# Hybrid decoder trunk on one core: the root's table load, a unit's end ahead of the weights' low part, and the attention's first loads at other slots

## The reference

```python
h = rmsnorm(x, g_pre) * (1 + scale) + shift          # scale, shift, gate from c @ w_ada
p = h @ w_in                                         # 1024 x 8704, split by columns
y_pool = pool_mixer(a_in, ...) * silu(a_g)
y_hgrn = hgrn2_mixer(b_q, b_f, b_i, ...) * silu(b_g)   # o = rmsnorm(o, norm_g) at its end
y_conv = short_conv_mixer(c_x, c_b, c_c, conv_w) * silu(c_g)
y_diff = diff_attention(d_q, d_k, d_v, ...) * silu(d_g)
merged = sum(sigmoid(m_g[n]) * (y_n @ w_merge_n) for n in range(4))
x = x + gate * rmsnorm(merged @ w_out, g_post)

# diff_attention, for each of 4 heads and each block of 128 queries
p = softmax(where(mask, q @ k.T * scale, NEG))       # two maps, m = 0 and 1
a = p[0] - lam_full * p[1]
o = rmsnorm(a @ v, norm_g) * (1 - lam_init)
```

## Time and profile before

| | us |
|---|---|
| median of 3 runs | 2526.8 |
| lowest, highest | 2520.53, 2531.47 |
| profiled execution | 2521.85 |
| its span, first to last instruction | 2520.0 |

### The profile page before, as it was taken

How to read it: one execution, slowest core, us unless ns; L and a number is a source line. 1 busy time by engine, 2 the same in 40 slices (tenths; PEclk the granted TensorE clock), 3 DMA queues, 4 the chain that set the end, 5 groups by cost and what they waited for, 6 DMA issues and landing times. The chain is left out here.

```text
span 2520.0 us, 35158 instructions
## 1 busy us (share of the span) xinstructions
PE 2264.2 (90%) x11572; PEld 1863.6 (74%) x11572; DVE 1429.2 (57%) x2638; ACT 1143.3 (45%) x2400; POOL 822.4 (33%) x739
## 2 busy tenths in 40 slices
PE   3598799898999889899999999999999967899998
PEld 2486677777777668687888888878888846677776
DVE  5676566655887777412776666445555434444452
ACT  3553455544544544422666666433434233434341
POOL 0113223323745654300232222123434216243342
PEclk7899999999999989999999999999999978999999
DMA  6699877758767666989564664487777777587781
GB/s 228 255 351 333 260 227 244 227 195 284 267 241 254 233 223 243 336 269 270 175 189 145 176 178 153 150 264 245 235 234 250 216 237 188 163 196 188 171 212 59
DMA packets 383963, 564.75 MB, mean 224 GB/s; under 512 B 32432, under 2 KB 248880, under 8 KB 382768
## 3 DMA queue, kind: packets, MB, share of 16 engines
q1 hardware_dynamic: 315248, 313.01, 42.8%
q10 hardware_dynamic: 68544, 249.59, 28.5%
HBM read 331.28 MB, written 231.21 MB: 223 GB/s over the span
## 5 line engine op out<-in xcount | busy, mean ns | idle before, releaser
L1682 PE MATMUL gb<-h_hi,w_both 128*128 128x512 f32 x1904 | 785.9, 413 | 89.2 <-ACT o L949 40.8
L1684 PE MATMUL gb<-h_hi,w_both 128*128 128x512 f32 x1904 | 755.1, 397 | 0.0
L1683 PE MATMUL gb<-h_lo,w_both 128*128 128x512 f32 x1904 | 754.0, 396 | 0.0
L1682 PEld LDWEIGHTS gb<-h_hi,w_both 128*128 128x128 f32 x1904 | 365.1, 192 | 173.0 <-issue 94.0
L1684 PEld LDWEIGHTS gb<-h_hi,w_both 128*128 128x128 f32 x1904 | 364.2, 191 | 80.8
L1683 PEld LDWEIGHTS gb<-h_lo,w_both 128*128 128x128 f32 x1904 | 365.7, 192 | 66.5
L949 ACT ACTIVATE o<-gb 128x512 f32<-128x512 f32 x272 | 161.5, 594 | 368.0 <-PE gb L1684 312.6
L809 POOL TENSOR_TENSOR C_prob<-C_prob,C_cf 128x512 f32<-128x512 f32 (+3 forms) x160 | 157.2, 1007 | 502.1 <-DVE C_cf L1358 488.1
L1014 ACT ACTIVATE C_prob<-C_sc,C_negm 128x512 f32<-128x512 f32 (+3 forms) x320 | 198.7, 622 | 245.4 <-DVE C_negm L1336 237.6
L1250 DVE TENSOR_TENSOR o<-gb,o 128x512 f32<-128x512 f32 x204 | 140.3, 688 | 228.7 <-PE gb L1684 218.0
L1240 DVE TENSOR_TENSOR w_both<-w,w_both 128x512 fp32r<-128x512 f32 x170 | 142.0, 836 | 173.4 <-ACT w_both L922 173.2
(11 more groups left out here) (230 smaller groups left out, 3711.7 us busy)
## 6 DMA issues: line engine op xcount, KB each, us to landing
wS_scratch<-w_both ACTq DMA_DIRECT2D x238, 512.0 KB, 4.4
w_both<-wS_scratch ACTq DMA_DIRECT2D x238, 512.0 KB, 4.3
w<-in_w_in_dram SPq DMA_DIRECT2D x68, 512.0 KB, 5.2
gT_scratch<-o SPq DMA_DIRECT2D x128, 256.0 KB, 4.7
D_gate<-gT_scratch SPq DMA_DIRECT2D x32, 1024.0 KB, 9.7
pT_scratch<-o SPq DMA_DIRECT2D x80, 256.0 KB, 4.2
C_qt<-qB_scratch SPq DMA_DIRECT2D x128, 128.0 KB, 3.6
C_ks<-kT_scratch SPq DMA_DIRECT2D x48, 256.0 KB, 5.7
```

Of the source, the lines that this page charges most:

```text
L1682: mm(to, hi[:, k, :], h_hi[j][:, k, :], start=(fresh and k == 0), stop=False, skip_group_check=True)
L1683: mm(to, hi[:, k, :], h_lo[j][:, k, :], start=False, stop=False, skip_group_check=True)
L1684: last = mm(to, lo[:, k, :], h_hi[j][:, k, :], start=False, stop=(k == KH - 1), skip_group_check=True)
```

## The change

Three edits, all in the first half. SyncE's five parts of the attention's first loads go from slots 45 to 49 to slots 39, 41, 43, 45 and 47 (the second half's stay). ScalarE's `root_h` gets an explicit load of the set with Ln and Exp for blocks 0 to 7, and `logs` drops its own for blocks 2 to 7. VectorE's end of a unit moves, within its slot, from behind `low(n+3)` and what follows it to directly ahead of `low(n+3)`, for the first step that the slot lists.

```diff
+BEGIN = ((39, 2), (279, 1))
...
                 for half in range(HALVES):
-                    if 0 <= n - ATTENTION[half][0] + 5 < 5:
-                        begin_attention(half, n - ATTENTION[half][0] + 5)
+                    part, odd = divmod(n - BEGIN[half][0], BEGIN[half][1])
+                    if not odd and 0 <= part < 5:
+                        begin_attention(half, part)
...
                 if i:
                     act.wait_ge(fin_done, i)
+                if i < MIX_HALF:
+                    act.preload_act_table_set("natural_log_exp_and_others")
                 link(a(rs[:, :, :], b7[:, 2:4, :], ACT.Ln, bias=epsb[:, :]))
...
                 i = mix_step(n, -9)
                 if i is not None:
-                    act.preload_act_table_set("natural_log_exp_and_others")
+                    if not 2 <= i < MIX_HALF:
+                        act.preload_act_table_set("natural_log_exp_and_others")
                     logs(i)
...
+            def end_units(half, s):
+
+                i = finished(half, s, 1)
+                if i is not None:
+                    factors(i)
+                i = None if half else finished(half, s, GATE)
+                if i is not None:
+                    gate_out(i)
+                i = finished(half, s, ON)
+                if i is not None:
+                    normalise(i)
...
+                taken = [hs for hs in att_slot(n)[:1] if hs[0] == 0]
+                for half, s in taken:
+                    end_units(half, s)
                 if n + LEAD < KEPT:
                     low(n + LEAD)
...
                 for half, s in att_slot(n):
-                    i = finished(half, s, 1)
-                    if i is not None:
-                        factors(i)
-                    i = None if half else finished(half, s, GATE)
-                    if i is not None:
-                        gate_out(i)
-                    i = finished(half, s, ON)
-                    if i is not None:
-                        normalise(i)
+                    if (half, s) not in taken:
+                        end_units(half, s)
                     z = piece(half, s)
```

## The result

The changed kernel takes 2482.21 us (median of 4 runs, 2480.70 to 2485.43); the kernel before took 2523.66 us beside it (4 runs, 2519.43 to 2531.47). The ratio is 0.9831, 95% interval 0.9818 to 0.9845: 41.5 us less. The profiled executions have spans of 2480.7 and 2520.0 us, 39.3 less. The forecast was 2488 with 2473 to 2509; measured against the 2526.8 it started from, the ratio gives 2484. So the total came out nearly as forecast. Its terms came out less well, as the stages show.

The account below looks back on a forecast made before the run. TensorE (PE), busy 90% of the span and working in program order, was taken as the bound. Gains of 10 + 7 + 22 = 39 us brought the median from 2526.8 to 2488 us, range 2473 to 2509.

Parts of the forecast that it names:

- Part 1: Slots 39 to 50: earlier first loads end PE's wait for causal_r in slot 50; -10 us, bounds -13 and +4.
- The 3 us put back for the collision: Slots 39 to 50: transfers moved earlier take 40 us where PE needs 37, so 3 us of the gain are lost.
- SyncE reaches the later kT stores when their `o` is ready: Slot 50: the store no longer queues behind loads, so 10.8 us of wait and 2.3 of clock, 13.1 us, can go.
- a wait under 1 us: Slot 50: the sign of the loads' move working, PE's wait for causal_r under 1 us, with full clock through the slot.
- Part 2: First half's mixers: one table load less ahead of the root shortens PE's stalls; -7 us, bounds 0 and -18.
- Part 3: First half's attention: a unit's end ahead of low removes PE's waits for y_out and on; -22 us, bounds -27 and +6.
- the sum over the 25 waits: First half's attention: idle time ahead of low plus low, against PE's wait; 25.5 of the 27.1 us go.
- for whatever comes late next: First half's attention: 3.5 us taken off the gain of the unit's end move for the next late result.
- Collision: Before slot 50: earlier loads fill the DMA engines and PE stands there instead; part 1 gives nothing, 2500 us; chance 0.14.
- Loop: First half's attention: ScalarE and VectorE, not PE, set the pace; part 3 gives 8 of its 22, 2502 us; chance 0.12.
- Interface: First half's attention: GpSimd's multiply stretches low by at most 1.0 us in 32 units; 2515 us; chance 0.06.
- Slower: First half's attention: y_out waits for PE's turn_back and holds VectorE's later work, 1.1 us a step; 2566 us; chance 0.04.

Follow-up runs that it names:

- only_a: The kernel before with only the attention's first loads moved to slots 39 to 47; 2518.33 us, ratio 0.9975.
- the five executions: Five profiled executions that run the changed kernel's very program up to the end of slot 50; slots 39 to 50 take 41.3 to 43.7 us.
- only_b: The kernel before with only the table loads changed: one load at the root, six left out at logs; 2514.05 us, ratio 0.9958.
- only_c: The kernel before with only a unit's end moved ahead of low in the first half's attention; 2492.55 us, ratio 0.9874.
- early_mask: The changed kernel with VectorE's two copies at the attention's beginning (ident_r, causal_r) in slot 47 instead of 50; 2478.99 us, ratio 0.9811.
- the fillers: The changed kernel with idle maxima added on VectorE: two behind low, two ahead of the unit's end, or one behind low; ratios 1.0047, 0.9940, 0.9906.
- outputs_ahead: The changed kernel with only y_out and on ahead of low, the factors behind it again; ratio 0.9845.
- fill_one: The changed kernel with one idle maximum on VectorE behind low in each of the 52 steps that end something; ratio 0.9906.
- root_only: The changed kernel with the six table loads at logs put back; 2476.57 us, ratio 0.9815.
- bunch39: The changed kernel with the attention's first loads one a slot at 39 to 43, not every second slot; 2482.13 us, ratio 0.9823.
- its half: The changed kernel with only the factors ahead of low, y_out and on behind it; ratio 0.9872.

## Why the prediction was right, and where its terms were not

**What bounds the kernel** held. Nothing gained in the first half was given back in a wait of the second: its attention took 440.8 us against 439.7.

**Part 1, forecast -10, measured -5.0** (6.8 in `only_a`, whose time fell by 6.3 us, 0.0025 of 2526.43; 6.8 as well between the mean of the five executions, 42.1, and that of the three with the old order, the kernel before, `only_b` and `only_c`, 48.9). The 3 us put back for the collision are about right: slots 39 to 49 take 35.8 us in the mean of the five and 32.4 in that of the three. The failed step is "SyncE reaches the later kT stores when their `o` is ready", taken to end the whole wait and bring the clock back with it, 13.1 us of slot 50's 17.1. SyncE does reach them in time (the store goes out at 261.52, as VectorE's `o` is done, 260.82 and 0.68), and slot 50 gives 11.5 us in four of the five. Two terms were left out: VectorE's own work ahead of the mask copy, 1.45 us of PE's wait in those four, and the two buffers of `hb`, which in the changed kernel's profile (5.4 us to landing) leave 3.59 of the 10.80 us, with the clock in slot 50 at 0.82, not 1. The prediction's own sign for this, a wait under 1 us, failed in all five. `early_mask` shows that the wait in slot 50 can be had; whether part of it comes back in slot 46 (3.53 us there, 1.22 to 3.30 in the five) its one profile doesn't tell.

**Part 2, forecast -7, measured -8.5** (6.3 in `only_b`). The forecast lies in the middle of what the stage shows: the kernels with part 2 take 446.2 to 449.5 us in it, the three without it (the kernel before, `only_a`, `only_c`) 454.6 to 455.8. The mechanism is as put: one load of 1283 ns ahead of the root, and nothing on PE's path at `logs`. PE's waits for ScalarE's copies in this stage fell by 7.9 us, the kernel before and then the changed one:

```profile
PE gb L1682 <- ACT o L949: 13.6, 6, 3.6
PE gb L1696 <- ACT o L952: 5.7, 5, 2.3
```

The loads of the changed kernel by line in its mixers (before: 8 at each of the three places), and two rows of PE's timeline behind roots:

```profile
L1111 ACT ACT_TABLE_LOAD x8 | 10.3, 1283 | 0.2
L1215 ACT ACT_TABLE_LOAD x2 | 2.6, 1283 | 0.0
```

```profile
651.52 0.53 PE L1696 MATMUL gb<-h_hi,w_both 128*128 128x512 f32 x1 [2.28 <-ACT o L952]
...
896.91 0.47 PE L1696 MATMUL gb<-h_hi,w_both 128*128 128x512 f32 x1 [3.40 <-DVE o L1256]
```

The first stall fell from 3.55 to 2.28 us, by 1.27. Not every stall that was counted moved: the one at 938.51, 3.40 us for VectorE, is 3.40 still, while the one a product ahead of it fell from 2.52 to 1.10. The Trainium skill's 2.66 us for a switch ("ScalarE: Activation LUTs", What ACT_TABLE_LOAD costs) would have made 14 us by the prediction's count; the first stall shows one load and no drain behind it, and the stage agrees with 1.28 a load.

**Part 3, forecast -22, measured -32.0.** The step that failed is a term of the sum. The idle time went as the sum over the 25 waits had it: PE's idle time of at least 0.1 us in this stage fell from 27.5 to 1.7 us, by 25.8, where the prediction had 25.5. Then it took 3.5 us off "for whatever comes late next"; nothing came. And it left out that PE's work gets shorter too: 261.18 us busy became 254.97 for the same 1412 matmuls. Of these 6.2 us some 1.8 are the clock. After the longest wait, 2.89 us to 533.28, it fell in the kernel before (columns as in the earlier trace rows):

```profile
530.00:535.00 5.00, 2.11 (x13) 1.65 (x12) 2.72 (x7) 1.67 (x3) 0.08 (x1) 0.94 0.61 232
535.00:540.00 5.00, 5.00 (x23) 4.19 (x23) 1.21 (x3) 1.16 (x3) 0.00 (x0) 0.71 0.66 220
```

A granted clock of 0.71 over 5 us is 2.9 us at the lower level of the two (1.2 of 2.4 GHz); 0.94 over the 5 us before is 0.6 more. In these 3.5 us half the work is done, so 1.8 are lost. The changed kernel has 1.00 over the whole stage. The other 4.4 us are the restarts, below. 3.5 + 6.2 + 0.3 = 10, the whole of the miss.

**Rivals.** Collision: real in its place, but about 3 us, which the sum had in it, and not all of part 1. Loop: as forecast, that it would leave 8 of 22, no; but the loop stands right behind PE's pace, as the fillers and `outputs_ahead` show: it cost 8.4 us with the factors left where they were, and `fill_one`, with 35.2 us in the loop, keeps just 9.3 of the 32.0. Interface: `low` went from 750 to 830 ns (42 of them) and from 692 to 812 (16), 5.3 us of VectorE in the stage, under the 0.85 us that was to speak for it. The 16 go with part 3 (812 in `only_c`, 691 in `only_a`); of the 42 most doesn't, as they take 797 in `only_a`, without part 3. The growth is in the direction of what the Trainium skill says of GpSimd and VectorE's instructions with two SBUF inputs ("GPSIMD Engine Reference", Key points), but no run separated that cause. PE shows nothing of it, as `low` wasn't late. Slower: excluded by 1.1 us of idle time in front of 32 `C_y_out`.

That 2488 lay 4 us from 2484 is partly luck: part 3 was 10 us short and part 2 1.5, part 1 5 too high, and stretches that weren't changed took 6.2 us more in this execution, 2.7 of them before slot 39. Part 1 in turn came out nearer to its forecast in the other four executions.

## What to carry to other kernels

When an engine in program order stands for a result, sum over its waits the smaller of the wait and the work that the result can be moved ahead of, what stands in front of it in its own group included; that sum met both the whole move (25.5 and 25.8 us) and its half (12.4 and 13.2), and each wait gone gives its restart on top. That a loop shows hardly a wait doesn't mean it has slack: here it stood behind the waits that were removed, and 35 us of added work in it cost 22.7. Where two causes hide each other so, the gains of the halves don't add up to that of the whole, and neither is a cause's share. Work that is off the path, as the six table loads, can be removed for tidiness but not for time.

## What the runs showed of the hardware

- A wait of PE costs more than its length. Without the clock's 1.8 us, PE's busy time fell by 4.4 us as its waits of 0.1 us or more for the outputs went from 25 to 2, 0.19 us each. Measured directly, from the start of the instruction before the wait to that of the fifth behind, less the wait, against the same sequences without a wait in the kernel before: 0.17 us more at `C_on` (10 with, 20 without) and 0.23 at the values (7 with, 25 without).
- The same program differs from execution to execution by stage: slots 0 to 38, the same program in all the kernels here (the fillers' have one memset more), took 164.0 to 168.1 us. A difference of 2 us in one stage of one profile is not a finding. The gain of part 3 is one: 31.6 to 32.4 us in the five kernels that have all of it and nothing added in its stage (the changed one, `only_c`, `early_mask`, `root_only`, `bunch39`). So is that of part 2, with 5.4 to 8.7 us.
- The time to landing of one store differs between orders of issue and between executions: the kT<-hb that slot 50 hangs on took 7.9 us behind four q loads, 6.3 and 8.2 in `only_b` and `only_c` with the same order, and with the loads spread 5.4 in the changed kernel and 2.6 to 3.3 in the four others that run the same program there. Why it took 5.4 in one of the five wasn't found.
